# Gate and up products with the tokens stationary, in groups of 512 columns; a retiled value stage; the decays spread over a round

## The reference

```python
x = x + rmsnorm(mix, g_mix_post[l])
h = rmsnorm(x, g_ffn_pre[l])
ff = (jax.nn.silu(h @ w_gate[l]) * (h @ w_up[l])) @ w_down[l]
x = x + rmsnorm(ff, g_ffn_post[l])
```

## Time and profile before

| | us |
|---|---|
| median of 3 runs | 1244.68 |
| lowest, highest | 1243.56, 1252.18 |
| the profiled execution | 1253.2 |
| its span, first to last instruction | 1251.5 |

### The profile page before, as it was taken

How to read it: one execution, slowest core, us unless ns; L and a number is a source line. 1 busy time by engine, 2 the same in 40 slices (tenths; PEclk the granted TensorE clock), 3 DMA queues, 4 the chain that set the end, 5 groups by cost and what they waited for, 6 DMA issues and landing times.

```text
span 1251.5 us, 17492 instructions
## 1 busy us (share of the span) xinstructions
PE 1226.7 (98%) x6551; PEld 1052.8 (84%) x6551; DVE 760.4 (61%) x983; ACT 618.4 (49%) x817; POOL 12.4 (1%) x35
## 2 busy tenths in 40 slices
PE   8999989999999999999999999999999999999997
PEld 7788878888888888888888888888888888888886
DVE  5555567767686655766666656656666654444544
ACT  5644557474564644654444454444444443444432
POOL 1000010000000000000000000000000000000000
PEclk9999989999999999999999999999999999999999
DMA  7677687867887555365565565565555565555551
GB/s 207 214 225 149 145 177 163 168 157 157 206 172 189 202 195 188 123 202 192 179 199 187 182 201 180 189 200 176 194 193 181 196 228 185 193 201 194 186 192 67
DMA packets 185925, 229.42 MB, mean 183 GB/s; under 512 B 5920, under 2 KB 145440, under 8 KB 185376
## 3 DMA queue, kind: packets, MB, share of 16 engines
q1 hardware_dynamic: 185600, 226.84, 61.8%
q0 software_dynamic: 288, 2.10, 0.4%
HBM read 226.82 MB, written 2.10 MB: 183 GB/s over the span
## 4 chain that ended last, share of the span: by engine, by line
PE 87%; DMA 7%; DVE 3%; ACT 1%; SPq 1%; issue 1%; DVEq 0%; ACTq 0%
PE bank L1031 86%; DMA raw<-in_w_in 7%; DVE w_lo L646 1%; ACT w_hi L398 1%; DVE h2T L653 0%; DVE resid L924 0%; PE bank L1173 0%; SPq L307 0%; SPq L295 0%; DVE gT L794 0%; DVE gT L804 0%; DVE pre L794 0%; ACT L515 0%; DVE probs L822 0%; DVE h L739 0%
## 5 line engine op out<-in xcount | busy, mean ns | idle before, releaser
L646 DVE TENSOR_TENSOR w_lo<-raw,w_hi 128x1024 fp32r<-128x1024 f32 x424 | 517.5, 1225 | 428.3 <-ACT w_hi L398 425.1
L398 ACT ACTIVATE w_hi<-raw 128x1024 fp32r<-128x1024 f32 x424 | 446.8, 1059 | 519.6 <-PE bank L1031 460.3
L1031 PE MATMUL bank<-h2T,w_hi 128*128 128x512 f32 x1408 | 488.9, 394 | 1.7 <-issue 1.6
L1031 PE MATMUL bank<-h2T,w_lo 128*128 128x256 f32 x1408 | 390.2, 277 | 0.0
L1031 PEld LDWEIGHTS bank<-h2T,w_hi 128*128 128x128 f32 x1408 | 264.0, 188 | 63.8 <-issue 1.8
L1031 PE MATMUL bank<-hT,w_hi 128*128 128x512 f32 x768 | 273.8, 400 | 1.1 <-DVE w_lo L646 1.0
L1031 PEld LDWEIGHTS bank<-h2T,w_lo 128*128 128x128 f32 x1408 | 264.2, 188 | 0.0
L1031 PE MATMUL bank<-w_hi,ffT 128*128 128x512 f32 x704 | 217.0, 389 | 0.0
L1031 PE MATMUL bank<-hT,w_lo 128*128 128x256 f32 x768 | 215.4, 280 | 0.0
L1031 PEld LDWEIGHTS bank<-hT,w_hi 128*128 128x128 f32 x768 | 145.3, 189 | 34.3 <-issue 1.3
L1031 PEld LDWEIGHTS bank<-w_hi,ffT 128*128 128x128 f32 x704 | 132.1, 188 | 27.6
(11 more groups left out here) (159 smaller groups left out, 584.1 us busy)
## 6 DMA issues: line engine op xcount, KB each, us to landing
raw<-in_w_in SPq DMA_DIRECT2D x64, 1024.0 KB, 15.7
raw<-in_w_gate SPq DMA_DIRECT2D x44, 1024.0 KB, 5.1
raw<-in_w_up SPq DMA_DIRECT2D x44, 1024.0 KB, 5.0
raw<-in_w_down SPq DMA_DIRECT2D x44, 1024.0 KB, 5.0
raw<-in_w_out SPq DMA_DIRECT2D x16, 1024.0 KB, 5.2
resid<-in_x SPq DMA_DIRECT2D x2, 1024.0 KB, 6.0
out<-resid SPq DMA_DIRECT2D x8, 256.0 KB, 2.5
g_post<-in_g_mix_post POOLq DMA_DIRECT2D x1, 1024.0 KB, 6.2
```

What stands on the lines that cost most here:

```text
L398: act.activation(w_hi[:, s % AHEAD, :], raw[:, s // 2, (s % 2) * SUB:(s % 2 + 1) * SUB], ACT.Copy).then_inc(hi_done, 1)
L646: dve.tensor_tensor(w_lo[:, s % AHEAD, :], raw[:, s // 2, (s % 2) * SUB:(s % 2 + 1) * SUB], w_hi[:, s % AHEAD, :].bitcast(F32), ALU.subtra ...
L1031: return pe.matmul(out_, lhsT, rhs, start=start, stop=stop, skip_group_check=True)
```

## The change

- **Gate and up** are computed by `sub_tokens`, in 11 groups of 512 columns (one round of gate, one of up, each 8 subs of two k tiles). A token is a partition, so the norm is the scale of ScalarE's Silu (`gate_silu`) and of VectorE's product with up (`gated`); results lie in `ff`, tokens on partitions. TensorE turns each group with eight transposes (`turned_ff`), in the next group's first round after its second sub (for the last group in the down stage's), and ScalarE and VectorE split the turned result into `ffT` (`turned_hi`, `turned_lo`). TensorE waits for `silu_done` and `ff_ready` before it writes the accumulators again; before the down stage it waits for both of the last group.
- **The value stage**: a sub is one k tile by 1024 columns (`sub_value`), with 4 KB rows in the loads where there were 2 KB. It starts with two tiles of `hT`; tiles 4 to 7 follow, and tiles 8 to 15 are turned between its products.
- **The ten small loads** are issued by ScalarE, ahead of its other work.
- **The decays** of the mLSTM heads are computed at subs 1, 2, 3, 6 and 7 of round R_IN + 1, and scores, weighted values and turned results each wait for the decays that free their bank.
- Before gate's first sub two tiles of `h2T` are awaited and not four; its later chunks are split inside the first round.

```diff
-PAIRS = D_FF // 256
-R_DOWN = R_FF + PAIRS
+FF_GROUPS = D_FF // 512
+R_DOWN = R_FF + 2 * FF_GROUPS
...
+DECAY_HEADS = {1: (0, 1), 2: (2,), 3: (3,), 6: (4, 5), 7: (6, 7)}
...
-    return {0: range(4), 2: range(4, 8), AHEAD: range(8, KT)}.get(s, ())
+    return {0: range(2), 2: range(2, 4), AHEAD: range(4, 8)}.get(s, ())
...
+def later_tiles(s):
+    return range(s + 7, s + 9) if s % 2 and s < 8 else ()
...
-        ff_g = sb("ff_g", [P, 2, SEQ], stack=ffn)
-        ff_u = sb("ff_u", [P, 2, SEQ], stack=ffn)
+        ff = sb("ff", [P, TT, 512], stack=ffn)
...
             for r in range(4):
                 for q in range(4):
-                    col = 2 * DH + (r % 2) * 512 + (r // 2) * COL_RET
-                    load(r, q, rows(w_in, 4 * q, 4, col, 512), wait=r > 0)
+                    load(r, q, rows(w_in, 8 * (r % 2) + 2 * q, 2, 2 * DH + (r // 2) * COL_RET, 1024),
+                         wait=r > 0)
...
-            with sp.Fori(0, PAIRS) as i:
-                for q in range(4):
-                    load(i + R_FF, q, rows(w_gate if q < 2 else w_up, 8 * (q % 2), 8, 256 * i, 256))
+            with sp.Fori(0, FF_GROUPS) as i:
+                for n, w in enumerate((w_gate, w_up)):
+                    for q in range(4):
+                        load(2 * i + (R_FF + n), q, rows(w, 4 * q, 4, 512 * i, 512))
...
+            for src, r0, n in ((g_mix_pre, C_GPRE, 16), (g_ffn_pre, C_GFFN, 16),
+                               (conv_b, C_CONVB, 16), (g_mlstm_head, C_GHEAD, 8),
+                               (g_ret_head, C_GHEAD + 8, 8)):
+                act.dma_start(right[r0:r0 + n, 0, 0:P], src[0, :].rearrange("(r c) -> r c", c=P))\
+                  .then_inc(small_in, 16)
...
-                    if rnd == R_IN + 1 and 2 <= s < 5:
-                        for h in range(3 * s - 6, min(3 * s - 3, HEADS)):
+                    if rnd == R_IN + 1:
+                        for h in DECAY_HEADS.get(s, ()):
                             mlstm_decay(h)
...
+            def gate_silu(i):
+                for t in range(TT):
+                    act.activation(ff[:, t, :], acc(0)[:, t, :], ACT.Silu,
+                                   scale=stat[:, S_RSTD + t:S_RSTD + t + 1]).then_inc(silu_done, 1)
+            def turned_hi(i):
+                act.wait_ge(ffT_full, i + 1)
+                for b in range(2):
+                    act.activation(ffT[:, bass.ds(4 * i + 2 * b, 2), 0:SEQ],
+                                   bank[:, B_FF + b, :].rearrange("p (k c) -> p k c", c=SEQ),
+                                   ACT.Copy).then_inc(ff_hi, 1)
...
+            def gated(i):
+                dve.wait_ge(sub_done, 16 * i + 8 * (R_FF + 2))
                 for t in range(TT):
+                    dve.wait_ge(silu_done, 2 * i + (t + 1))
+                    dve.scalar_tensor_tensor(ff[:, t, :], acc(1)[:, t, :],
+                                             stat[:, S_RSTD + t:S_RSTD + t + 1], ff[:, t, :],
+                                             ALU.mult, ALU.mult).then_inc(ff_ready, 1)
+            def turned_lo(i):
+                for b in range(2):
+                    dve.wait_ge(ff_hi, 2 * i + (b + 1))
+                    two_tiles = ffT[:, bass.ds(4 * i + 2 * b, 2), :]
+                    dve.tensor_tensor(two_tiles[:, :, SEQ:2 * SEQ],
+                                      bank[:, B_FF + b, :].rearrange("p (k c) -> p k c", c=SEQ),
+                                      two_tiles[:, :, 0:SEQ].bitcast(F32), ALU.subtract).then_inc(ff_lo, 1)
...
+            def sub_value(e, k):
+                pe.wait_ge(lo_done, 16 * e + k + 1)
+                slot = k % AHEAD
+                for t in range(TT):
+                    hi_x = hT[:, k, t * P:(t + 1) * P]
+                    lo_x = hT[:, k, SEQ + t * P:SEQ + (t + 1) * P]
+                    for c in range(2):
+                        o, w = acc(2 * e + c)[:, t, :], slice(512 * c, 512 * (c + 1))
+                        mm(o, hi_x, w_hi[:, slot, w], k == 0, False)
+                        mm(o, hi_x, w_lo[:, slot, w], False, False)
+                        ins = mm(o, lo_x, w_hi[:, slot, w], False, k == KT - 1)
+                ins.then_inc(sub_done, 1)
...
+            for k in range(KT):
+                pe.wait_ge(xT_lo, k + 1)
+                sub_value(0, k)
+                if k % 2 and k < 8:
+                    pe.wait_ge(h_ready, CHUNKS * TT)
+                    pe.wait_ge(xT_lo, k + 1)
+                    for t in range(TT):
+                        transposed(h0, t, 4 + k // 2, first_bank)
+            for k in range(KT):
+                sub_value(1, k)
...
-                pe.wait_ge(decay_ready, 2 * HEADS)
+                pe.wait_ge(decay_ready, HEADS + 2)
...
+            def turned_ff(i):
+                for t in range(TT):
+                    pe.wait_ge(ff_ready, 2 * i + (t + 1))
+                    for j in range(4):
+                        c = (j % 2) * SEQ + t * P
+                        ins = pe.transpose(bank[:, B_FF + j // 2, c:c + P], ff[:, t, j * P:(j + 1) * P], ident)
+                ins.then_inc(ffT_full, 1)
+            def ff_sub(i, n, s):
+                sub_tokens(16 * i + (8 * (R_FF + n) + s + 1), s % AHEAD, h2T, n, 2 * s, KT - 1)
...
+            for n in range(2):
+                pe.wait_ge(acc_free, E_FF + n + 1)
+                for s in range(8):
+                    if n == 0:
+                        pe.wait_ge(xT_lo, KT + 2 * s + 2)
+                    ff_sub(0, n, s)
+                    if n == 0 and s == 1:
+                        chunk_transposed(2)
+                    if n == 0 and s == 3:
+                        pe.wait_ge(xT_lo, KT + 4)
+                        chunk_transposed(3)
+            pe.wait_ge(xT_lo, 2 * KT)
+            with pe.Fori(1, FF_GROUPS) as i:
+                pe.wait_ge(silu_done, 2 * i)
+                for s in range(8):
+                    ff_sub(i, 0, s)
+                    if s == 1:
+                        turned_ff(i - 1)
+                pe.wait_ge(ff_ready, 2 * i)
+                for s in range(8):
+                    ff_sub(i, 1, s)
+            pe.wait_ge(silu_done, 2 * FF_GROUPS)
+            pe.wait_ge(ff_ready, 2 * FF_GROUPS)
```

More of the change, by code:

```diff
@@ L434, in v_round @@
                     ahead(r, s)
+                    if first:
+                        transposed_hi(hT, C_GPRE, 0, first_bank, later_tiles(s))
                     if first and s == 7:
@@ L592, in ffn_pair, with mid_hi @@
-            def ffn_pair(i, first=False):
+            def mid_hi(c):
+                transposed_hi(h2T, C_GFFN, KT // 2, mid_bank, range(4 * c, 4 * c + 4))
+            def gate_silu(i):
[8 more added lines that the diff above has]
+                                   ACT.Copy).then_inc(ff_hi, 1)
@@ L606, in ffn_pair @@
-                    if s == 7:
-                        copy_right(1, 2 * i + (E_FF + 1))
-                        act.wait_ge(ff_ready, i + 1)
-                        act.activation(ffT[:, bass.ds(2 * i, 2), 0:SEQ], ff_u[:], ACT.Copy)\
-                           .then_inc(ff_hi, 1)
-            ffn_pair(0, first=True)
-            with act.Fori(1, PAIRS) as i:
-                ffn_pair(i)
-            square_root_table()
+                    if not first and s == 2:
+                        turned_hi(i - 1)
@@ L1010, in _ @@
+            ff_rounds(0, first=True)
+            dve.wait_ge(norm2_ready, 1)
+            with dve.Fori(1, FF_GROUPS) as i:
+                ff_rounds(i)
+            gated(FF_GROUPS - 1)
+            for s in range(8):
+                lo(R_DOWN, s + AHEAD)
+                if s == 2:
+                    turned_lo(FF_GROUPS - 1)
             for g in range(4):
                 full, end = divmod(DOWN_SUBS * (g + 1) - 1, 8)
-                with dve.Fori(3 * g, full) as r:
+                with dve.Fori(max(3 * g, 1), full) as r:
```

287 lines of the change are left out of this document (132 added, 155 removed).

## The result

| | before | after |
|---|---|---|
| median of 12 runs each, us | 1243.55 | 1256.84 |
| lowest, highest | 1242.72, 1253.39 | 1253.83, 1260.26 |
| the profiled execution | 1253.2 | 1257.24 |
| its span | 1251.5 | 1255.5 |

The ratio is 1.0092, with an interval of 1.0076 to 1.0109: slower by 13.3 us. That is still within 1%, but 13 us above the forecast and outside its range. The two profiled executions are only 4.0 us apart, since the one of before is one of its long ones.

The account below looks back on a forecast made before the run. TensorE was taken as the bound, busy for 1226.7 of 1251.5 us. Value stage -2.3, projections 0, norm stage -0.9 and gate and up +2.2 gave -1.0 us, a median of 1243.7 us; range 1238 to 1252.

Parts of the forecast that it names:

- the pace: Gate and up: 2112 products 0.2267 us apart, 704 fewer products than before, a gain of 9.9 us.
- blocks of transposes: Gate and up results turned on TensorE: 11 blocks of eight at 1.0 us, +11.0 us, ends 9.6 and 12.3.
- Rival 3: Each transpose in gate and up blocks TensorE for its recorded 0.273 us: 14 us more, 1257.7; 0.06 together with rival 4.
- rival 4: TensorE waits for gated at every gate and up group's start: +15 us, 1258.7; chance 0.06 together with Rival 3.
- the norm stage: Before the first gate sub, two tiles of h2T split instead of four: -0.9 us.
- the value stage's own part: Value stage: load stalls go, -4.4 us, and 16 moved transposes come onto the path, +2.1; -2.3 us.
- the start: Time to the first value product: 0 taken, ends -1.3 and +2 (coefficients' small loads arrive late and hold VectorE).
- the late squares: At the start, ScalarE reaches its squares 1.3 us later, behind ten load issues, and the norm and hT follow.
- the one new wait: Ahead of the down products TensorE waits for the last gated: 2 x 0.69 us plus two hand-overs, +1.5 us.
- the projections: Projections with the heads: kT ready 2.5 us earlier but meeting the same load landing; 0 taken, ends -10.8 and +4.
- rival 2: The feed of w_in falls behind as everything in the first third moves against the loads: 1247 to 1253; chance 0.15.
- rivals 1 and 5: First: the heads' stalls go too, 1239 to 1240, chance 0.10; second: much faster, with no room for 1232, chance 0.03.

Follow-up runs that it names:

- e2: The kernel after with the wait for the last group's ff_ready moved from ahead of the first down group to ahead of the second; 1254.38 us (1.0039 of before).
- e1: The kernel after with the ten small loads back on SyncE's queue, ahead of its first raw load; 1254.88 us (1.004 of before).
- e3: The kernel after with the eight decays together again at subs 2, 3 and 4; 1255.77 us (1.0045 of before).
- e5: The kernel before with the change's start and value stage alone; 1253.01 us (1.0018 of before).
- e7: The kernel after with small loads back on SyncE, last ff_ready wait moved later and four filling products taken out; 1250.13 us (0.9991 of before).
- e8: The kernel before with only the decays spread over subs 1, 2, 3, 6 and 7; 1251.31 us (1.0014 of before).
- e13: The kernel before with the projections' 48 loads reading w_out in place of w_in; 1241.92 us.
- e12: The kernel after with the projections' 48 loads reading w_out in place of w_in; 1249.73 us.
- e6: The kernel after, unedited, run again on the same chip as before at 1251.34 us; 1260.26 us (1.0068 of before).
- e4: The kernel before with the change's gate and up stage, norm stage and wait ahead of down alone; 1255.54 us (1.0032 of before).

## Why the prediction was wrong

**Right: the pace.** Gate and up products start 0.2267 us apart, and the whole stage from first to last product is 1.7 us shorter (-0.3 forecast). The blocks of transposes cost 0.90 us each (e2), not 1.0, so that 11 of them give back 9.9 us, just what the 704 fewer products save. Rival 3 (0.273 each) is out, and so is rival 4: no group waits inside the loop, TensorE being busy for 489.84 of 489.90 us.

**Right: the norm stage** (-0.7 for -0.9) **and the value stage's own part.** Its stalls went and the moved transposes came, -2.3 as forecast, in after, e1, e3 and e5.

**Wrong: the start, "I take 0", with +2 as its far end.** It measured +5.2. The mechanism of that far end was the right one, small loads that land late and hold VectorE before its second half of x, and its size was not: the coefficients are turned 4.1 us later, and 7.6 us instead of 6.5 pass from there to the first product. Two things add up. The small loads share the DMA engines with the first raw loads. And TensorE, idle meanwhile, works on at half clock, behind filling products that had been free (1.5 us from e1 to e7). The term that the sum did price, the late squares, came true (1.75 us) and cost nothing, since it lies inside the wait for the coefficients.

The trace after shows the two queues at once, which no row of before did. This is from the DMA part of the kernel after, 0 to 16 us: queue, packets, MB, share of the 16 engines.

```profile
q1 hardware_dynamic: 1004, 4.90, 78.6%
q10 hardware_dynamic: 528, 0.20, 4.9%
```

Of this, 8 to 13 us:

```profile
q1 hardware_dynamic: 393, 1.53, 80.8%
q10 hardware_dynamic: 360, 0.14, 10.4%
```

The 0.2 MB of ScalarE's queue (q10), issued by 6.04 us, lasted until 14.1; on SyncE's queue the same loads, issued by 6.40, were there at 10.05.
**Wrong: "the one new wait", +1.5.** It measured +4.0, and 1.7 more for the clock (1.5 to 2.7 over six traces). The step counted what gated takes (2 x 0.69, measured 1.40) but not what stands ahead of it on VectorE: a w_lo whose w_hi is released by the very same event. The text had even used this fact, a w_hi that waits for the next sub's end, to argue that the w_lo *behind* gated loses nothing; at the boundary it stands in front. And a clock fall was priced in the projections from the earlier trace rows, but not here, although there a wait of 3.09 us had cost 1.6. e2 shows both at once: -5.7 us.

**Not settled in the number, short in the reading: the projections, 0 (-10.8 to +4).** The two traces have -3.1, with one of before's long executions on one side. The argument was that a product that runs earlier meets the same landing; e8's trace shows that, with one wait turned into another. But the reading of the stalls was short: they are owed to how w_in lands. In the first comparison before had a typical time near what e13 has (1243.55 against 1241.92, so projections of about 298 us, worked out by that difference), and the kernel after was 7.1 us above e12 (about 302), which is past the far end of +4 if it holds. So of the 13.3 us in the result some 5.5 are not the change's own work but its meeting with the loads of w_in; this split is worked out over two sets and is not shown by a run. It is rival 2's mechanism, given 0.15, on top of the two misses, and not instead of them. In the later sets before had this loss itself, and the change then cost 8.9 us (e6).

**In the sums, without weight.** 11 blocks at 1.10 us are 12.1 us and not 12.3, and twice 1.6 us of lost clock are 3.2 and not 3.4. Both stand only in far ends, the second in rivals 1 and 5 as well.

**Open.** Why w_in lands as it does is not settled. The runs changed the array, and with it the distance of rows, their alignment and the place in memory all together. The arrays whose loads land early have rows 8192 B (w_out, w_down) and 22528 B (w_gate, w_up) apart, both multiples of 256 B; w_in's, 32832 B, is none, but it is also the longest. The Trainium skill, "DMA: Bandwidth & Descriptors", section How a descriptor splits into AXI transactions, says that a piece not starting at a multiple of 256 B costs extra beats, since its first transaction begins at the boundary below. Rows 32832 B apart start at multiples of 64 B, three of four off those boundaries. For these a fifth transaction beside four, 1.25 times as many, or 2 to 6 beats beside 32, would be an estimate from that page. The engines' share here rose 1.4 times (0.77 against 0.55), more than either, and landings three times later and irregular need something beside it. No run here tells alignment from the rest. It also stays open why before escapes this loss in one set and not in the others, and by what means loads with rows of 4 KB hold up the small loads ahead of them by a microsecond and more; that they do is the difference between the five traces and the six at e1.

## What to carry to other kernels

When a new wait is priced, write down for the waited-for engine everything that stands ahead of the awaited operation and is released by the same event: here that made 1.4 us into 3.8, and the idle time took the clock with it for 1.5 to 2.7 more. Put such a wait at the first instruction that needs it, not at the stage's border. Loads that are few and small but awaited early must be asked for ahead of the large ones, on the same queue, since beside them, on a queue of their own, they came 4 us later here. And where two delays end at the same wait, price the later one: the late squares cost nothing here.

## What the runs showed of the hardware

- Small loads of 0.2 MB on a second queue beside 1 MB loads were complete at 13.8 to 14.4 us (six traces), on the first queue ahead of these at 10.1 to 10.6 (six traces, 2 KB rows behind them) or 11.1 to 12.3 (five traces, 4 KB rows).
- Ten load issues took ScalarE from 0.81 to 6.04 us, 0.28 to 1.10 us each, and its table load waited for them.
- The same 3.8 us of idle time cost 1.5 to 1.7 us by the clock in three traces and 2.5 to 2.7 in three others. In the kernel after the granted clock still read 1.00 in the idle stretch and 0.60 over the next 4.3 us; in e4 it read 0.79 in the idle stretch already. Behind the 5.57 us of idle time at the start it was 0.50 for more than 5 us.
- 1 MB loads in 1 KB pieces: median landing 5.3 us after issue from w_out's rows, 5.1 from w_gate's, 15.6 from w_in's (120 to 400 us of before), at 170 to 190 GB/s.
